# A decoder trunk on one core: x laid out by the host, and the first norm's squares summed by TensorE from pairs that VectorE added

## The reference

```python
def rms_norm(x, g):
    xf = x.astype(jnp.float32)
    y = xf * lax.rsqrt(jnp.mean(xf * xf, axis=-1, keepdims=True) + EPS)
    return (y * g.astype(jnp.float32)).astype(x.dtype)

def swiglu(h, w_gate, w_up, w_down):
    return (jax.nn.silu(h @ w_gate) * (h @ w_up)) @ w_down

def half_ffn(x, i, k):
    h = rms_norm(x, norm_g[i, 2 * k])
    return x + 0.5 * swiglu(h, ffn_w_gate[i, k], ffn_w_up[i, k], ffn_w_down[i, k])
```

## Time and profile before

| what | value |
|---|---|
| runs of before | 2060.96 us median (2057.55 to 2062.87) |
| the profiled execution | 2060.5 us, of it a span of 2058.9 us |
| PE busy | 2038.1 us, 99% of the span |
| DVE, ACT, POOL busy | 78%, 55%, 18% |
| DMA | mean 144 GB/s |

### The profile page before, as it was taken

How to read it: one execution, slowest core, us unless ns; L and a number is a source line. 1 busy time by engine, 2 the same in 40 slices (tenths; PEclk the granted TensorE clock), 3 DMA queues, 4 the chain that set the end, 5 groups by cost and what they waited for, 6 DMA issues and landing times.

```text
span 2058.9 us, 44454 instructions
## 1 busy us (share of the span) xinstructions
PE 2038.1 (99%) x16716; PEld 1991.5 (97%) x16716; DVE 1608.6 (78%) x2686; ACT 1124.1 (55%) x1948; POOL 364.3 (18%) x437
## 2 busy tenths in 40 slices
PE   9999999999999999999999999999999999999999
PEld 8999999999999999999999999998779999999999
DVE  7779985426467898998899898668776578989998
ACT  6446554433134665655665565446676456656555
POOL 0011111222011111111111111112333221111111
PEclk9999999999999999999999999999999999999999
DMA  5467773231314777876677777543322126777775
GB/s 167 120 159 178 189 195 117 82 102 63 103 63 124 166 178 178 194 184 152 158 182 182 185 183 183 136 133 84 115 73 83 62 62 156 183 178 180 181 179 153
DMA packets 360763, 295.70 MB, mean 144 GB/s; under 512 B 22111, under 2 KB 325260, under 8 KB 360356
## 3 DMA queue, kind: packets, MB, share of 16 engines
q1 hardware_dynamic: 323706, 227.26, 36.7%
q0 software_dynamic: 36592, 66.07, 19.6%
q10 hardware_dynamic: 314, 0.37, 0.1%
HBM read 224.57 MB, written 2.66 MB: 110 GB/s over the span
## 4 chain that ended last, share of the span: by engine, by line
PE 85%; DVE 6%; DMA 5%; issue 2%; ACT 2%; SPq 0%; POOL 0%; DVEq 0%; ACTq 0%; POOLq 0%
PE side L856 28%; PE main L807 26%; PE main L856 20%; DMA raw<-raw 2%; PE side L1390 1%; DMA sums_w<-raw 1%; DVE w_lo L2150 1%; PE main L1139 1%; PE main L1307 1%; PE side L1227 1%; PE side L1349 1%; PE side L1055 1%; PE main L1207 1%; DMA raw<-in_ffn_w_up 1%; DMA raw<-in_ffn_w_gate 1%
## 5 line engine op out<-in xcount | busy, mean ns | idle before, releaser
L856 PE MATMUL side<-xw_hi,w_hi 128*128 128x260 f32 x1344 | 380.8, 283 | 5.0 <-ACT main L1572 2.0
L856 PE MATMUL side<-xw_hi,w_lo 128*128 128x260 f32 x1344 | 381.1, 284 | 0.0
L856 PE MATMUL side<-xw_lo,w_hi 128*128 128x260 f32 x1344 | 380.2, 283 | 0.0
L2150 DVE TENSOR_TENSOR w_lo<-raw,w_hi 128x512 fp32r<-128x512 f32 (+2 forms) x472 | 324.8, 688 | 35.3 <-ACT w_hi L1517 17.4
L856 PE MATMUL main<-xw_hi,w_hi 128*128 128x260 f32 x1008 | 286.1, 284 | 0.0
L856 PE MATMUL main<-xw_lo,w_hi 128*128 128x260 f32 x1008 | 284.7, 282 | 0.0
L856 PE MATMUL main<-xw_hi,w_lo 128*128 128x260 f32 x1008 | 284.5, 282 | 0.0
L856 PEld LDWEIGHTS side<-xw_hi,w_hi 128*128 128x128 f32 x1344 | 253.2, 188 | 7.7 <-ACT main L1572 2.8
L856 PEld LDWEIGHTS side<-xw_hi,w_lo 128*128 128x128 f32 x1344 | 253.2, 188 | 0.0
L856 PEld LDWEIGHTS side<-xw_lo,w_hi 128*128 128x128 f32 x1344 | 252.8, 188 | 0.0
L3091 POOL DMA_DIRECT2D sums_w<-raw x116 | 100.7, 868 | 687.8 <-DMA raw<-in_ffn_w_gate 314.8
(11 more groups left out here) (464 smaller groups left out, 5422.4 us busy)
## 6 DMA issues: line engine op xcount, KB each, us to landing
sums_w<-raw POOLq DMA_DIRECT2D x112, 256.0 KB, 3.3
raw<-raw POOLq DMA_DIRECT2D x112, 256.0 KB, 5.1
raw<-in_ffn_w_gate SPq DMA_DIRECT2D x86, 256.0 KB, 4.6
raw<-in_ffn_w_gate SPq DMA_DIRECT2D x43, 512.0 KB, 5.9
raw<-in_ffn_w_up SPq DMA_DIRECT2D x84, 256.0 KB, 3.9
raw<-in_ffn_w_up SPq DMA_DIRECT2D x42, 512.0 KB, 6.2
raw<-in_gmlp_w_in SPq DMA_DIRECT2D x16, 1024.0 KB, 5.4
raw<-in_ffn_w_down SPq DMA_DIRECT2D x56, 256.0 KB, 4.0
```

The costliest lines, as they stand in the source:

```text
L856: mm = nc.tensor.matmul(into[j], w_tiles(w, weights_at(s, j))[:, k, :], moving[:, k, order[j], :], start=(j in (0, 1) and k == 0 and i == ...
L2150: a = nc.vector.tensor_tensor(dst, src, hi.bitcast(F32), ALU.subtract)
```

## The change

- The host hands over x already in the kernel's layout (`x_rows`, 128 x 8 x 520) and all small vectors as one array of 103 columns (`vector_cols`). SP loads x straight into `x` in five pieces (tiles 0, 1, 2-3, 4-5, 6-7), between them the gate weights in pieces (tile 0 from ACT's queue, then 1, 2-3, 4-5, 6-7), then the up weights in two halves, and last the constants. All transposes of x, the sample tokens and the vectors go, and with them DVE's copies.
- ACT squares the tiles of x as they lie (`first_square`, into `first_squares`). DVE adds them in pairs for tiles 0 to 5 (`add_pair`). PE sums the pairs and tiles 6 and 7 over the partitions by float32 products with a 128 x 128 matrix of ones (`sum_squares`, two matmuls of 260 columns each, five times: two inside `first_pair`, ahead of tiles 4 and 6, and three in `first_sums`, ahead of chunk 1). That leaves the sum on all partitions, and `spread_first` goes.
- ACT takes the root of that 128 x 520 result, and DVE makes `rstd_all` by a reciprocal of 128 x 520, in the place of the copy.
- ACT's first table load is for Sqrt, in the place of Copy. `BUSY` is 11, before 12.

```diff
-            load_x(0)
-            load_first(0, 2, first_in[0])
-            for dst, src in vector_sources()[:6]:
-                sp.dma_start(dst, src).then_inc(vectors_in, 16)
-            load_x(1)
-            load_first(2, 4, first_in[1])
-            load_x(2)
-            load_first(4, KD, raw_in[0])
-            load_x(3)
+            load_x(0)
+            load_first(0, ffn_w_gate[0, 0], 1, 2, first_in[1])
+            load_x(1)
+            load_first(0, ffn_w_gate[0, 0], 2, 4, first_in[2])
+            load_x(2)
+            load_first(0, ffn_w_gate[0, 0], 4, 6, first_in[3])
+            load_x(3)
+            load_first(0, ffn_w_gate[0, 0], 6, KD, raw_in[0])
+            load_x(4)
+            load_first(1, ffn_w_up[0, 0], 0, 4, second_in)
+            load_first(1, ffn_w_up[0, 0], 4, KD, raw_in[1])
+            sp.dma_start(const[:], table[:, 0:N_CONST]).then_inc(const_in, 16)
...
+                def first_sums():
+                    pe.wait_ge(piece_lo, KD)
+                    pe.wait_ge(pair_added, 3)
+                    sum_squares(KD - 3)
+                    pe.wait_ge(tile_squared, KD - 1)
+                    sum_squares(KD - 2)
+                    pe.wait_ge(tile_squared, KD)
+                    sum_squares(KD - 1)
...
                         first_pair()
-                        spread_first()
                         for m in range(2):
                             before = {}
                             if m == 0:
-                                before = {0: lambda: pe.wait_ge(piece_lo, KD), 2: lambda: pe.wait_ge(piece_lo, KD + 1),
+                                before = {0: first_sums, 2: lambda: pe.wait_ge(piece_lo, KD + 1),
                                           4: lambda: pe.wait_ge(piece_lo, KD + 2), 6: lambda: pe.wait_ge(lo_done, 2)}
+                            else:
+                                pe.wait_ge(const_in, 16)
...
                     pe.wait_ge(xg_lo_done, k + 1)
+                    if k >= 4 and k % 2 == 0:
+                        pe.wait_ge(pair_added, k // 2 - 1)
+                        sum_squares(k - 3)
...
-                    if k + 3 < KD:
-                        turn_x(k + 3)
...
+            def sum_squares(k):
+
+                for half in range(2):
+                    mm = nc.tensor.matmul(side[:, 2 + half, 0:HALF], square[:, 0, 0:P],
+                                          first_squares[:, k, half * HALF:(half + 1) * HALF],
+                                          start=(k == 1), stop=(k == KD - 1), skip_group_check=True)
+                if k == KD - 1:
+                    mm.then_inc(rms_mm, 1)
...
+            first_split(0, 1)
             first_gain(0)
+            first_split(1, 2)
             first_gain(1)
...
+            for k in range(2, KD, 2):
+                first_split(k, k + 2)
+                first_gain(k)
+                first_gain(k + 1)
+                first_square(k - 2)
+                first_square(k - 1)
+            first_square(KD - 2)
+            first_square(KD - 1)
             second_split(0)
...
+            act.wait_ge(rms_mm, 1)
+            nc.scalar.activation(halves(root[:, :]), side[:, 2:4, 0:HALF], ACT.Sqrt, scale=1.0 / D,
+                                 bias=eps[:, 0:1]).then_inc(root_done, 1)
...
                     if n == 0:
-                        dve.wait_ge(rms_mm, 1)
-                        nc.vector.tensor_copy(halves(rstd_all[:, :]), side[:, 2:4, 0:HALF]).then_inc(rstd_done, 1)
+                        dve.wait_ge(root_done, 1)
+                        nc.vector.reciprocal(rstd_all[:], root[:]).then_inc(rstd_done, 1)
                         dve.wait_ge(rstd_done, 1)
...
+            def add_pair(k):
+                dve.wait_ge(tile_squared, k + 2)
+                nc.vector.tensor_tensor(first_squares[:, k + 1, :], first_squares[:, k + 1, :], first_squares[:, k, :],
+                                        ALU.add).then_inc(pair_added, 1)
...
+            for k in range(KD):
+                first_rest(k)
+                if k >= 3 and k % 2:
+                    add_pair(k - 3)
+            for k in range(0, KD, 2):
+                second_rest(k)
```

More of the change, by code:

```diff
@@ L469, in program @@
         at_ffn = [None] * 4
-        at_ffn[0] = At(tile=KD, evac=KD)
+        at_ffn[0] = At()
         at_ffn[0].groups = FIRST_GROUPS
@@ L863, in token_sums @@
                     pe.wait_ge(sum_done, at.sums)
[L864 to L868 removed]
+                    sum_tokens(rms_mm)
+                def first_sums():
[6 more added lines that the diff above has]
+                    sum_squares(KD - 1)
                 def spread():
[L871 removed]
+                    pe.wait_ge(first_scales, 3 * at.spread + 3)
                     spread_scales(spread_done)
@@ L931, in ffn @@
                         n, e, l, h = n + 4, e + 8, l + 5, h + 2 * pairs
-            def turn_x(k):
-                if k % 2 == 0:
-                    pe.wait_ge(x_in[k // 2], 16)
-                if k >= 2:
-                    pe.wait_ge(evac_done, k - 1)
-                for q in range(QB):
-                    t = nc.tensor.transpose(side[:, k % 2, q * P:(q + 1) * P], x_tok[:, q, k * P:(k + 1) * P], ident)
-                t.then_inc(tile_done, 1)
             def first_pair():
@@ L1457, in _ @@
         def _(act):
-            act.dma_start(const[:, 0:P], table[:, 0:P]).then_inc(start_in, 16)
-            act.dma_start(xs_tok, x_sample[:, 0, :]).then_inc(start_in, 16)
-            for dst, src in vector_sources()[6:]:
-                act.dma_start(dst, src).then_inc(vectors_in, 16)
-            act.dma_start(const[:, P:], table[:, P:N_CONST]).then_inc(const_in, 16)
+            act.dma_start(raw[:, 0, 0:WC], w_rows(ffn_w_gate[0, 0])[:, 0, 0:WC]).then_inc(first_in[0], 16)
+            act.dma_start(vectors[:, 0:n_vec], vector_cols).then_inc(vectors_in, 16)
             act.wait_ge(begin_set, 2)
-            nc.scalar.activation(primed[:, 0:1], eps[:, 0:1], ACT.Copy)
+            nc.scalar.activation(primed[:, 0:1], eps[:, 0:1], ACT.Sqrt)
             def split_ahead(n0, i, s, t, width=SLOT):
@@ L2234, in token_scales @@
             def token_scales(at):
-                first = 3 * at.spread + 3
+                first = 3 * at.spread
                 dve.wait_ge(root_done, at.rms + 1)
@@ L3258, in _, with rows_of, laid_out @@
             ffn(at_ffn[3], at_end, True)
-INPUTS = ("x_prompt", "x_sample", "cache_mla", "page_table", "norm_g", "ffn_w_gate", "ffn_w_up", "ffn_w_down",
-          "gmlp_w_in", "gmlp_b_in", "gmlp_v_norm", "gmlp_w_s", "gmlp_b_s", "gmlp_w_out",
-          "mla_w_dq", "mla_q_norm", "mla_w_uq", "mla_w_dkv", "mla_kv_norm", "mla_w_uk", "mla_w_uv",
-          "mla_qk_gain_q", "mla_qk_gain_k", "mla_w_o")
+def rows_of(a):
+    return np.asarray(a).reshape(-1, P).T
+def laid_out(inputs):
+    tokens = np.concatenate([inputs["x_prompt"][0], inputs["x_sample"][:, 0]], axis=0)
+    gains = [inputs[f"mla_qk_gain_{n}"][0] for n in "qk"]
+    vectors = [rows_of(inputs[n]) for n in ("norm_g", "gmlp_b_in", "gmlp_v_norm", "mla_q_norm", "mla_kv_norm")]
+    vectors += [rows_of(g[:NOPE]) for g in gains] + [rows_of(np.concatenate([g[NOPE:], g[NOPE:]])) for g in gains]
+    return dict(x_rows=tokens.reshape(TOK, KD, P).transpose(2, 1, 0), vector_cols=np.concatenate(vectors, axis=1))
+INPUTS = ("cache_mla", "page_table", "ffn_w_gate", "ffn_w_up", "ffn_w_down", "gmlp_w_in", "gmlp_w_s", "gmlp_b_s", "gmlp_w_out",
+          "mla_w_dq", "mla_w_uq", "mla_w_dkv", "mla_w_uk", "mla_w_uv", "mla_w_o")
 OUTPUTS = ((P, KD, TOK), (1, 1, SEQ, CD), (1, NS, 1, CD), (1, NS, 1, GM))
```

163 lines of the change are left out of this document (47 added, 116 removed).

## The result

The changed kernel takes 2064.87 us (median of 13 runs, 2059.90 to 2070.86), the kernel before, run beside it, 2060.35 (13 runs, 2057.55 to 2064.10). The ratio is 1.0018, with a 95% interval of 1.0010 to 1.0026: 2.1 to 5.4 us longer. That is inside the forecast's range of 2056.5 to 2066.0 and 3.4 us above its number. It lies above the ends that its terms add up to (2064.1) and above the 2059 to 2064 that it gives its own case. It is also within the 0.3% that the forecast took for what cannot be told from no change, though 13 runs of each do tell it: the interval leaves 1 out.

A forecast was written before the change was run, and what follows sets the result against it. PE bounds the kernel, busy for 2038.1 of 2058.9 us. From 2060.5, -0.9 for chunk 2's start and +1.7 for the half clock give 2061.3, by the median 2061.8; forecast 2061.5, range 2056.5 to 2066.0.

The forecast's parts named there:

- its own case: Forecast of a longer pause ahead of chunk 2 and a half clock behind it: 2059 to 2064 us, chance 0.48.
- Step 1: Kernel start: first tile of x lands at 5.0, so PE's first product comes at 7.3, 3.6 us earlier.
- Step 2: From first product to chunk 1: 15.9 us of PE work plus 1.0 of waits; chunk 1 at 24.2, 3.8 earlier.
- Step 3: Root and reciprocal delay `scaled`: pause ahead of chunk 2 grows from 1.3 to 4.2 us; chunk 2 at 40.0.
- Step 4: Behind the pause ahead of chunk 2, PE's clock falls to half for 3.4 us: 1.7 lost, ends 0 and 3.4.
- rival A: The longer pause ahead of chunk 2 comes but the clock stays full: 2059.6 us, 2060.1 by the median; chance 0.27.
- the -0.9 for chunk 2's start: Sum's term for PE starting chunk 2 at 40.0 against 40.94 before; ends -2.8 to +0.2 us.
- B: The pause ahead of chunk 2 does not grow, all 3.8 us stay: 2056.7, 2057.2 by the median; chance 0.08.
- C: ACT and late x pieces slow `first_pair`: chunk 1 no earlier than 26, chunk 2 at 41.8, 2064.8 us; chance 0.13.
- D: First tile lands no earlier than 5.44, PE starts near 7.7: costs 0.4 us, inside the forecast's range; no own chance.

The follow-up runs named there:

- early_fine: Changed kernel with chunk 2's weight split and the second up copy made earlier, and x's tiles 2 and 3 loaded as separate pieces: 2058.89 us, ratio 0.9991 to before.
- copy_rstd: Changed kernel with the 128x520 reciprocal replaced by a copy of the root (first norm left wrong): 2058.97 us, ratio 0.9990 to before.
- before_recip: Kernel before with its copy of the spread factors made a 128x520 reciprocal (first norm left wrong): 2066.18 us, ratio 1.0031 to before.
- warm_pause: Changed kernel with 17 unread float32 products of ones filling PE's pause ahead of chunk 2: 2060.38 us, ratio 0.9994 to before.
- before_look: Kernel before, unchanged, profiled again in one execution: 2066.26 us, mean clock 0.997.
- after_again: Changed kernel, unchanged, run a second time: 2063.86 us, ratio 1.0020 to before; its profiled execution took 2063.8.
- after_look1: Changed kernel, unchanged, first of three more profiled executions: 2064.18 us, mean clock 0.999.
- after_look2: Changed kernel, unchanged, second of three more profiled executions: 2063.97 us, mean clock 0.999.
- after_look3: Changed kernel, unchanged, third of three more profiled executions: 2064.29 us, mean clock 0.998.
- half_recip: Changed kernel with the first norm's reciprocal taken of 260 columns only, the other 260 copied as roots: 2061.08 us, ratio 1.0004 to before.

## Why the prediction was right, and what it had wrong

**Step 1, the first product.** Forecast 7.3, measured 6.94, and 6.4 to 6.6 in four later profiles. The landing that it rested on was taken too late, inside its ends (4.1 to 5.44 for 5.0): the first tile landed 3.4 us after its issue at 0.94, so at 4.3, and its weights, issued together with it by ACT, 3.6 after, at 4.5. The step's lower estimate of 4.2 was the nearer one. From 4.5 on the chain took 2.4, where 2.3 were added up. Right.

**Step 2, the way to chunk 1.** Forecast 24.2 with one wait of 1.0 for the third tile; measured 23.96 with a wait of 0.92 there, and 23.04 to 23.32 in the later profiles. The cause of that wait was right too: `early_fine`, which lets this tile land alone, has none.

**Step 3, the factor rstd.** Forecast: a pause of 4.2 in place of 1.3, chunk 2 at 40.0. Measured: 4.05 and 39.98, and 4.0 in every profile. The stretch did move as a whole (11.46 both times), and both `copy_rstd` (1.17 without it) and `before_recip` (3.88 with it) show it from their side.

**Step 4, the clock.** The mechanism was right: a half clock behind the new pause, in all five profiles of this kernel. `warm_pause` shows that it costs time of its own. The size was taken from one row, 3.45 us of half clock, as 1.7. It was 1.4 to 1.7 in four profiles and 2.6 in the fifth; and since the mean clock of 18 of the 28 executions is 0.998 or lower, as the fifth's, a value of about 2.3 would have been nearer (1.6 for ten and 2.6 for 18 make 2.2 in the mean, if the other 17 are like the one that was profiled). The rows held one such stretch and couldn't show that it may last twice as long; the upper end of 3.4, chosen for that case, took it in. The Trainium skill (TensorE: Matmul & The Clock Gate, Why this matters for your kernels) warns against pauses between bursts of matmuls; the traces agree, with a fall at every 4.0 us pause and none at 1.2 to 1.4. The other rule of the Trainium skill that the forecast weighed, that transposes don't count like products, was its ground for rival A. A is out, no execution of the changed kernel kept its clock, but no run here tests that rule itself.

**The sum, where the forecast missed.** The term that failed is the -0.9 for chunk 2's start. It set 40.0 against 40.94 of the profiled execution, and that 40.94 held 1.7 us of half clock which the text itself saw in the earlier trace rows but took for a property of the kernel. It is a property of the execution: 42 of 74 have none, and then chunk 2 starts near 39.2 by the estimate above. The changed kernel's five profiles have 39.98, 39.33, 39.05, 39.22 and 39.30, 39.4 in the mean. So for a typical execution steps 1 to 3 give +0.2, not -0.9. With 2.3 for the clock that is +2.5 against an execution of before without half clock, and some +1.2 against the mean of them all (their clocks of 0.999 and less come to 18 x 0.001 + 13 x 0.002 + 0.003 over 74, or 0.00064 of 2060 us, 1.3). The runs say +3.7 (2.1 to 5.4) and +4.1 (1.4 to 6.8). So even the mended sum stays below both intervals, and some 2.5 us of the measured 3.7 are not explained by it.

**What stays open.** The executions sorted by clock leave a rest too: the ten of the changed kernel at 0.999 take 2063.3 us in the mean, the 42 of before at 1.0 take 2060.1; of the 3.2 between them 0.2 and 1.6 are accounted for, and 1.4 are not. The 15 of the changed kernel at 0.998 take 2065.2; by 0.2 and 2.6 they should be 2.8 above 2060.1 and are 5.1 above it. Part of it may be the jitter far behind. The prediction said that it would be wrong if stretches far behind the first block differed by microseconds. They do, but between executions of the same code as well. This is the span behind the start of chunk 2, less the half clock in it, with PE's waits on line 842 (856 before):

| execution | span | start of chunk 2 | lost to half clock behind it | rest | those waits |
|---|---|---|---|---|---|
| before | 2058.9 | 40.94 | 0 | 2018.0 | 6.3 |
| `before_look` | 2064.6 | 42.41 | 1.7 | 2020.5 | 8.8 |
| `before_recip` | 2066.0 | 43.96 | 1.7 | 2020.3 | 8.2 |
| changed | 2058.3 | 39.98 | 1.6 | 2016.7 | 4.0 |
| `after_again` | 2062.2 | 39.33 | 1.4 | 2021.5 | 8.4 |
| `after_look1` | 2062.6 | 39.05 | 1.7 | 2021.9 | 8.0 |
| `after_look2` | 2062.3 | 39.22 | 1.6 | 2021.5 | 8.1 |
| `after_look3` | 2062.6 | 39.30 | 2.6 | 2020.7 | 8.2 |

The same instructions take from 2016.7 to 2021.9 us, and most of the difference is in those waits. In the mean the changed kernel's rest is 0.9 us longer than before's (2020.5 against 2019.6); whether that is real or only comes out so in five executions against three can't be said from them.

**The rivals.** A (pause, no fall) is refuted, B (no longer pause) too. C did not come: chunk 1 started at 23.96 at the latest in the five profiles, not after 26; that its time of 2064.8 is almost the measured 2064.87 is chance. D is out, the first product came at 6.94, not 7.7. That the range held the time is in part luck. The forecast had the pause and the half clock right, with 0.48 on them, but it expected +0.5 us and +3.7 came; the terms with their ends reach 2064.1, and only the room for C and for the spread of the runs carried the range past 2064.87.

## What to carry to other kernels

Time won at the start of the bounding engine is worth only what the next engine in the chain lets through: here 3.1 of the 4.1 us that were won were given back because a root and a reciprocal of 3.4 us, behind which everything for the next chunk was queued, took the place of a 0.7 us copy, and the half clock at the longer pause took more than the 1.0 that was left. Where a long step has to be there, put the work for which PE waits ahead of those that only the later chunks need; in this kernel that was worth 4.5 us against the changed kernel, though not surely anything against the one before. And before comparing a forecast with a profile, read the granted clock of the profile's own start: what belongs to one execution must be taken out of the baseline.

## What the runs showed of the hardware

- The half clock at a pause of 4.0 us is not always as long: 3.4 us in four profiles, 6.8 in one. It can begin within the pause (at 37.7 in a pause from 35.2 to 39.3) or a microsecond after its end (`before_recip`, at full clock from 43.96 to 45.06). What of it lies in the pause costs nothing.
- At a pause of 2.73 us the mean clock was below 1.0 in eight of eleven executions, and the one profiled shows the fall. A pause of 2.5 us near the end of `before_look` has one as well, at 2050.7. At 1.17 and 1.38 it fell in none of the two profiles, and the mean clock was 1.0 in 21 of 23 executions. The longest pause without a fall in any profile is one of 2.15 us, late in the profile of `half_recip` (from 2044.9 to 2047.0).
- Float32 products of ones that nobody reads keep the clock up in a pause: 1.0 in nine of eleven executions.
- The dense new start of the changed kernel, products from 6.9 on with no transposes of x between them, had no half clock ahead of the pause in any of the eleven profiles of it and its variants. Before's start had one in all three profiles that hold it, though 42 of its 74 executions with a clock on record have a mean of 1.0.
- A reciprocal of 128 x 520 float32 values takes DVE 3.40 us, where a copy of as many takes 0.68 out of `side` and 0.43 out of `root` (`copy_rstd`); one of 128 x 260 takes 1.77 (`half_recip`).
